# Attention heads in a one-core transformer step: transposing the probabilities of head i-1 ahead of the scores of head i

## The chip, the cores and the metric

The kernel runs on one core of a Trainium2 chip. The metric is the device time of one execution in microseconds. The engines are named as the profile names them: PE is TensorE's matrix multiplication (PEld its weight load), DVE is VectorE, ACT is ScalarE, POOL is GpSimd, and SP is SyncE, which here only issues transfers. A queue name such as ACTq is the engine's sequencer.

## What is computed

One step of a backbone with two layers, float32 throughout. It has 128 prompt tokens (block 0) and 512 sample tokens (blocks 1 to 4 of 128 each), and both groups go through both layers. A layer is a mixer, which holds two kinds of attention, and an expert stage:

```python
q_na, k_na, v_na, p, q_mla, ckv, krope = branch_inputs(h, lp)
o_na  = nat_latent_attn(q_na, k_na, v_na, kc_na, vc_na, rel_bias)   # sample: window + 128 cached keys
o_mla = dense_block_attn(q_mla, concat([k_lat, k_ctx]), concat([v_lat, v_ctx]), MLA_QK ** -0.5)
x = x + g1 * (concat([o_na, o_pool, o_mla]) @ w_out)
h2 = modulate(rms_norm(x, norm2), sh2, sc2)
x = x + g2 * peer(h2, peer_wq, peer_subkeys, peer_u, peer_v)
```

Each attention has six heads. `mla` (latent) attention lets each of the 512 sample tokens see all 512 sample keys and 128 cached ones, so 640. `na` (neighbourhood) attention lets a sample block see the neighbouring blocks of keys and the cached one: 384 keys for blocks 1 and 4, 512 for blocks 2 and 3, with a bias and a mask added. The prompt sees only its own 128 keys in both. Softmax is exact: a maximum over the row, an exponential with its sum, and a division at the end. In `peer`, eight heads choose 16 of 16384 experts for each token. For every block, head and choice one row of `peer_u` and one of `peer_v` (4 KB each, for each of 128 tokens) are gathered from memory. There are 1280 such steps, called rows below.

## The kernel before

**One order for all engines.** `whole_order` (from line 352) writes the whole work as one list of steps, `plan`. Each engine walks this list and does its own part of each step, with semaphores between the engines. What stands later in the list never overtakes what stands earlier on the same engine.

**The expert rows.** A step `("row", r)` makes POOL gather row r+4 of `peer_u` and row r-16 of `peer_v` (line 931), four buffers each. DVE multiplies a `u` row with the tokens and sums it (L1604), and does one part of a later unit's top-k search. ACT scales a 128x128 identity by the weights (L1192, 18 rows behind). PE multiplies this diagonal with the `v` row of 20 rows before and adds it up in `expert_sum` (L1933, four matmul records). Every 16 rows (a unit) ACT also computes a gelu (L1182), and PE a score product for a later unit (L1909).

**The weave.** `weave` (line 322) mixes the mixer's steps between the rows. It gives each step an estimated cost and spreads the sum of costs evenly over the rows. `s` and `pt` have the same cost (1.0), `pv` has 0.6. Rows 51 to 73 hold the sample's latent heads and the neighbourhood heads of block 1 in layer 0, rows 704 to 720 those of layer 1. Neighbourhood heads of blocks 2 to 4 stand in rows 84 to 116 and 728 to 759. The prompt's heads stand ahead of all rows in layer 0, blended with modulation products (L1661), and one step at a time between rows 432 and 497 in layer 1.

**A head of attention** is three steps.
- `s`: PE computes the scores (`scores`, L1820, two products for 640 keys). DVE adds bias and mask (L1415 and L1419, `na` of the sample only) and takes the maximum (L1424). ACT computes the exponential with its sum into `prob` in SBUF (L1137), which frees the scores' bank.
- `pt`: PE transposes the probabilities, one 128x128 transposition for each key block (`turn_probs`, recorded at the helper's L1635). They go in one part, or for 640 keys in part 0 (four blocks) and part 1 (the fifth). DVE copies part 0 of the sample's latent heads (L1436), ACT copies all other parts (L1149) to `prob_T`.
- `pv`: PE multiplies the transposed probabilities with the values (`head_values`, L1850). Behind a block's sixth head DVE divides by the sums (L1446, L1449).

`prob` and `prob_T` have two buffers each. `attention` (line 265) puts the heads' steps in order.

**The PSUM banks.** `work` has four banks. `Banks.place` (line 129) walks the plan and gives each result one bank, or the pair (0, 1) or (2, 3) for scores of 640 keys. Among the spots that are empty at that point of the plan it takes the one that has been empty longest. PE waits for the previous holder of the bank to be freed before it writes (`empty`). A bank counts as empty for the plan once the step that uses it has passed, though the engine may still be reading it. `pv` holds one bank for all six heads of a block.

Of the kernel before, what the change touches and what calls it, by code (L numbers as in the profile page):

```python
# [264 lines left out]
def attention(l, items):  # L265

    out = []
    for i in range(len(items) + 2):
        if i < len(items):
            out += [("s", l, *items[i])]  # L270
        if 1 <= i <= len(items):
            out += [("pt", l, *items[i - 1])]
        if i >= 2:
            out += [("pv", l, *items[i - 2])]
    return out
# [62 lines left out]
def prompt_mixer(l):  # L338
    att = attention(l, items_of("mla", GROUP[0]) + items_of("na", GROUP[0]))
    return heads_of_prompt(l), att  # L340


def sample_front(l):
    return (norm1(l, 1) + heads_of_sample(l) + attention(l, items_of("mla", GROUP[1]))
            + [("lX", l, b) for b in GROUP[1]] + attention(l, items_of("na", TAILS[1])) + tail(l, 1))
# [1683 lines left out]
```

## Time and profile before

| | |
|---|---|
| median of 3 runs | 4815.94 us (4813.23 to 4818.26) |
| profiled execution | 4793.14 us, span 4791.3 us |
| granted TensorE clock, mean | 0.949 of full speed |
| PE busy | 3804.4 us (79%) |
| DVE busy | 2559.7 us (53%) |
| ACT busy | 963.8 us (20%) |
| POOL busy | 2571.6 us (54%) |
| chain that ended last | PE 41%, POOL 19%, DMA 19%, issue 12%, DVE 4%, ACT 2% |

The span is the profiled execution from its first to its last instruction. Busy time is time in which an engine worked, so the rest of its span is waiting or issuing. The chain is followed back from the last instruction: at each step to what released it, or to the instruction before it on its engine. A share is thus the part of the span in which that engine was what all else waited for. Since the stages have different limits, the rows below are by stage. The times in them are microseconds from the start of the span.

### The profile page before, as it was taken

How to read it: one execution, taken by the hardware profiler on the slowest of the kernel's cores; microseconds unless marked ns; L12 is line 12 of the kernel's file. 1: busy time of each engine (PE TensorE's matmuls, PEld its weight loads, DVE VectorE, ACT ScalarE, POOL GpSimd, SP SyncE). 2: the span in 40 equal slices, each digit the busy share in tenths (PEclk: the TensorE clock that was granted, in tenths of full speed). 3: DMA queues.
4: the chain of work that ended last, by engine and by line, in shares of the span. 5: the costliest groups of instructions: out<-in, count | busy, mean ns of one | idle time of the engine just before them, and what ended most of it. 6: DMA issues, size and time to landing. Idle time of an engine off the chain costs nothing.

```text
span 4791.3 us, 37649 instructions
## 1 busy us (share of the span) xinstructions
PE 3804.4 (79%) x10586; PEld 1719.4 (36%) x10586; DVE 2559.7 (53%) x6434; ACT 963.8 (20%) x2482; POOL 2571.6 (54%) x2833
## 2 busy tenths in 40 slices
PE   7877789998888787778777958899977777777777
PEld 2344455443232233333223435554422222222222
DVE  1253456654555556655564334475565666666552
ACT  1122222221111112211121112231211121111111
POOL 0045324555666666666664441255566666666665
PEclk8988899999999999999999978899999999999999
DMA  5565658889999999999997534598999999999998
GB/s 197 209 217 172 194 177 329 319 312 370 382 392 385 382 393 365 369 366 374 378 371 275 184 129 155 188 347 311 330 370 370 365 373 367 371 370 367 367 368 303
DMA packets 464499, 1505.24 MB, mean 314 GB/s; under 512 B 59908, under 2 KB 78632, under 8 KB 463784
## 3 DMA queue, kind: packets, MB, share of 16 engines
q0 software_dynamic: 368640, 1342.34, 75.3%
q1 hardware_dynamic: 95656, 160.50, 9.6%
q8 instruction: 90, 1.47, 0.1%
q14 instruction: 113, 0.93, 0.1%
HBM read 1496.99 MB, written 5.67 MB: 314 GB/s over the span
## 4 chain that ended last, share of the span: by engine, by line
PE 41%; POOL 19%; DMA 19%; issue 12%; DVE 4%; ACT 2%; another core or an unknown queue 2%; SPq 1%; DVEq 0%; ACTq 0%; POOLq 0%
PE expert_sum L1933 20%; POOL expert_rows L931 17%; DMA expert_rows<-in_peer_v,experts 13%; DMA expert_rows<-in_peer_u,experts 5%; PE work L1687 4%; PE work L1661 3%; PE work L1884 3%; PE work L1899 3%; PE work L1820 2%; PE work L1635 2%; PE work L1850 2%; POOL stat_rstd L878 1%; DVE expert_rows L1604 1%; PE work L1872 1%
## 5 line engine op out<-in xcount | busy, mean ns | idle before, releaser
L1933 PE MATMUL expert_sum<-expert_rows,weight_diagonals 128*128 128x512 f32 x5120 | 2548.3, 628 | 676.4 <-DMA expert_rows<-in_peer_v,experts 501.5
L1604 DVE CUSTOM_DVE_ANT_0 expert_rows<-expert_rows,tokens 128x1024 f32<-128x1024 f32 x1280 | 1559.0, 1218 | 1098.8 <-DMA expert_rows<-in_peer_u,experts 971.4
L931 POOL DMA_INDIRECT expert_rows<-in_peer_v,experts x1280 | 1223.4, 956 | 1379.3 <-PE expert_sum L1933 970.4
L1933 PEld LDWEIGHTS expert_sum<-expert_rows,weight_diagonals 128*128 128x128 f32 x5120 | 928.1, 197 | 2073.9 <-issue 1911.9
L931 POOL DMA_INDIRECT expert_rows<-in_peer_u,experts x1280 | 1213.7, 948 | 476.3 <-issue 355.6
L1192 ACT ACTIVATE weight_diagonals<-ident,expert_weights 128x128 f32<-128x128 f32 x1280 | 437.2, 391 | 611.2 <-issue 260.0
L1635 PE MATMUL work<-ident,scratch 128*128 128x128 f32 (+1 forms) x814 | 156.8, 320 | 237.1 <-DVE scratch L1274 69.2
L1687 PE MATMUL work<-weight_ring,h_or_mixed 128*128 128x384 f32 (+2 forms) x800 | 260.6, 480 | 4.2 <-DMA weight_ring<-in_w_in 2.4
L1635 PEld LDWEIGHTS work<-ident,scratch 128*128 128x128 f32 (+1 forms) x814 | 112.4, 159 | 312.4 <-DVE scratch L1274 77.9
L1687 PEld LDWEIGHTS work<-weight_ring,h_or_mixed 128*128 128x128 f32 x800 | 147.8, 196 | 115.9 <-issue 61.9
L1182 ACT ACTIVATE gelu_dots<-dots 128x16 f32<-128x16 f32 x80 | 17.3, 216 | 847.6 <-issue 428.6
L1661 PE MATMUL work<-weight_ring,silu_cond 128*2 128x512 f32 x384 | 176.5, 615 | 13.2 <-DMA weight_ring<-in_w_mod 11.7
L875 POOL TENSOR_SCALAR stat_biased<-stat_sums 128x6 f32<-128x6 f32 (+1 forms) x82 | 16.9, 207 | 311.0 <-DVE stat_sums L1293 115.2
L1424 DVE TENSOR_REDUCE neg_max<-work 128x1 f32<-128x640 f32 (+3 forms) x120 | 76.3, 637 | 180.5 <-PE work L1820 168.9
L1899 PE MATMUL work<-h_or_mixed,weight_ring 128*128 128x128 f32 (+1 forms) x768 | 149.6, 354 | 3.7 <-ACT h_or_mixed L1010 3.7
L1137 ACT ACTIVATE scratch<-work,neg_max 128x640 f32<-128x640 f32 (+3 forms) x120 | 77.3, 644 | 353.3 <-DVE neg_max L1424 295.0
L1884 PE MATMUL work<-weight_ring,scratch 128*128 128x512 f32 x320 | 140.6, 592 | 0.0
L1899 PEld LDWEIGHTS work<-h_or_mixed,weight_ring 128*128 128x128 f32 x768 | 112.9, 200 | 49.0 <-issue 19.4
L1176 ACT ACTIVATE topk<-topk 128x16 f32<-128x16 f32 x80 | 24.5, 306 | 482.5 <-issue 254.4
L1604 DVE DVE_READ_ACCUMULATOR2_ANT dots<- 128x1 f32 x1280 | 105.5, 82 | 0.0
L1461 DVE COPY scratch<-work 128x512 f32<-128x512 f32 x20 | 13.8, 692 | 163.1 <-PE work L1884 163.1
L1182 ACT ACT_TABLE_LOAD x78 | 100.1, 1283 | 1.4
(164 smaller groups left out, 2591.1 us busy)
## 6 DMA issues: line engine op xcount, KB each, us to landing
weight_ring<-in_w_mod SPq DMA_DIRECT2D x24, 2048.0 KB
weight_ring<-in_w_out SPq DMA_DIRECT2D x12, 2048.0 KB
weight_ring<-in_peer_wq SPq DMA_DIRECT2D x12, 2048.0 KB
expert_rows<-in_peer_u,experts POOLq DMA_INDIRECT x1280
expert_rows<-in_peer_v,experts POOLq DMA_INDIRECT x1280
weight_ring<-in_w_in SPq DMA_DIRECT2D x12, 1536.0 KB
weight_ring<-in_w_in SPq DMA_DIRECT2D x4, 2048.0 KB
weight_ring<-in_t_pool SPq DMA_DIRECT2D x4, 2048.0 KB
```

The source lines that it names most:

```text
L931: g.indirect_dma_start(ring[row % n], None, table, bass.IndirectOffsetOnAxis(ap=idx_st[:, col:col + 1], axis=0),).then_inc(row_in[row % n] ...
L1182: a_.activation(gel[:, e * TOPK:(e + 1) * TOPK], dots[:, e * TOPK:(e + 1) * TOPK], ACT.Gelu_apprx_tanh).then_inc(gelu_ready, 1)
L1192: a_.activation(diags[:, at * P:(at + 1) * P], ident[:, :], ACT.Copy, scale=wgt[:, col:col + 1]).then_inc(diag_ready, 1)
L1604: v_.tensor_tensor_reduce(out=u_ring[r % U_RING], in0=u_ring[r % U_RING], in1=tokens[:, :], scale=1.0, scalar=0.0, op0=ALU.mult, op1=ALU.a ...
L1635: ins = t_.transpose(dst[0:n, j * P:(j + 1) * P], v, ident[:, :])
L1661: ins = t_.matmul(dst[0:2, :], sct[:, :].rearrange("p (c k) -> p k c", c=2)[:, kk, :], wt[:, kk, :], start=kk == 0, stop=kk == KC - 1)
L1687: ins = t_.matmul(dst[:, 0:n], hT(b, kk), wt[:, kk, 0:n], start=kk == 0, stop=kk == KC - 1)
L1820: ins = t_.matmul(dst[:, col:col + n], lhs, keys[:, key0:key0 + n], start=True, stop=True)
L1850: ins = t_.matmul(dst[:, h * DH:(h + 1) * DH], prob_T[item_no[item] % 2][:, k, :], val, start=k == 0, stop=k == len(blocks) - 1)
L1884: ins = t_.matmul(dst, o_T[:, kk, :], wt[:, kk, :], start=kk == 0, stop=kk == KC - 1)
L1899: ins = t_.matmul(dst[:, 0:len(blocks) * P], wt[:, kk, (h % 4) * P:(h % 4 + 1) * P], h_blocks[:, blocks[0]:blocks[-1] + 1, kk, :], start=k ...
L1933: ins = t_.matmul(acc[:, hf * 512:(hf + 1) * 512], diags[:, at * P:(at + 1) * P], v_ring[row % V_RING][:, hf * 512:(hf + 1) * 512], start= ...
```

## The change

In `attention`, the step `pt` of head i-1 is put ahead of the step `s` of head i. It stood behind it. `pv` of head i-2 stays last. All engines that take part in these steps (PE, DVE, ACT) walk the new order. The planner `Banks` and the weave run on the new list.

```diff
     for i in range(len(items) + 2):
+        if 1 <= i <= len(items):
+            out += [("pt", l, *items[i - 1])]
         if i < len(items):
             out += [("s", l, *items[i])]
-        if 1 <= i <= len(items):
-            out += [("pt", l, *items[i - 1])]
         if i >= 2:
             out += [("pv", l, *items[i - 2])]
```

## Rows read from the trace of the kernel before

**Rows 1.** Windows by stage; columns in the first line, PEclk is the clock.
```profile
core 0: us, PE busy (x) PEld busy (x) DVE busy (x) ACT busy (x) POOL busy (x), PEclk, DMA share, GB/s
550.00:682.00 132.00, 106.39 (x529) 70.48 (x528) 67.11 (x139) 36.94 (x96) 34.09 (x36) 0.96 0.53 177
682.00:705.00 23.00, 22.36 (x120) 15.22 (x119) 17.59 (x45) 8.15 (x25) 9.47 (x10) 1.00 0.83 296
1100.00:2550.00 1450.00, 1140.75 (x2707) 449.77 (x2707) 849.58 (x2203) 278.88 (x729) 921.38 (x975) 0.97 0.99 377
2895.00:3032.00 137.00, 111.24 (x526) 75.01 (x525) 58.52 (x118) 33.33 (x91) 26.25 (x28) 0.86 0.42 136
3117.00:3214.00 97.00, 97.00 (x400) 57.33 (x398) 82.02 (x195) 36.98 (x96) 58.50 (x62) 1.00 0.96 352
```
**Rows 2.** Chain of waits, a latent round: start, duration, engine, result and line.
```profile
2959.75 0.84 DVE neg_max L1424
...
2961.61 0.33 PE work L1635
2961.94 1.07 PE work L1850 x10
2963.01 1.15 PE work L1820 x4
...
2964.18 0.84 DVE neg_max L1424
```
**Rows 3.** The same view, latent rounds with an expert row in layer 0.
```profile
574.16 1.72 PE expert_sum L1933 x4
575.88 0.55 PE work L1635 x5
...
578.66 0.84 DVE neg_max L1424
...
584.83 0.83 DVE neg_max L1424
...
590.98 0.84 DVE neg_max L1424
```
**Rows 4.** The same view: a copy-out behind a turn, and scores started from idle.
```profile
565.48 0.34 PE work L1635
...
565.90 0.28 ACT scratch L1149
...
661.11 1.33 PE work L1820 x4
```
**Rows 5.** The same view, neighbourhood heads of block 1, both layers.
```profile
684.15 0.86 PE work L1820 x7
...
687.36 0.55 PE work L1635 x3
...
703.24 1.77 PE expert_sum L1933 x4
...
3033.28 0.86 PE work L1820 x7
...
3056.78 2.19 PE work L1850 x12
```
**Rows 6.** The same view, neighbourhood heads of blocks 2 to 4, both layers.
```profile
766.30 1.07 PE work L1820 x4
...
769.38 1.28 ACT L1137
...
771.51 0.66 PE work L1635 x4
...
3133.31 0.84 PE work L1850 x8
...
3135.21 1.91 PE expert_sum L1933 x4
3137.12 0.44 PE work L1635 x4
```
**Rows 7.** The same view, prompt heads of layer 0 beside a modulation product.
```profile
162.66 0.30 DVE neg_max L1424
...
163.55 7.04 PE work L1661 x16
```

## The prediction

> **What bounds the kernel now.** I read the windows by stage first [rows 1]. Most of the span (1100 to 2550 us, and again after 3380) is paced by the expert rows' transfers: DMA share 0.99 with TensorE at 79%. The change touches only stages where heads of attention are computed, and these differ. The neighbourhood heads of sample blocks 2 to 4 fill TensorE: 97.00 of 97 us in layer 1. Those of block 1 do so in layer 0 (22.36 of 23 us). The latent (mla) heads of the sample leave it 20% idle with DMA share only 0.42 to 0.53. The prompt's heads of layer 0 stand between modulation products of 7 us [rows 7]. Then I read the chain of waits inside each stage.
>
> In a latent head the chain is serial [rows 2]: the max starts 0.02 us after the scores end, the first transposition stands 1.86 us later (max, exponential), then one transposition 0.33, ten value matmuls 1.07, the next scores 1.15: a round of 4.43 us. Only one transposition stands in the chain, because head i-1's fifth key block is turned into a PSUM bank that scores(i) hold (the planner has four banks; the value sum keeps one for six heads, scores of 640 keys take a pair). So part 1 of turn i-1 waits for exponential i, although its data has long been there. The other four transpositions run under the max.
>
> In the neighbourhood heads scores fit one bank, two heads are in flight, and the chain is TensorE alone. Each head gives it scores 1.06, transpositions 0.44, values 0.84, and rows of 1.72 to 1.91 us between [rows 6].
>
> **The change, part by part.** No instruction, transfer or wait is added or removed. All engines walk the same plan, so DVE (max, copy-out of part 0), ScalarE (exponential, copy-out) and TensorE all get the new order; SP and POOL have no attention step, and rows, gathers and weight loads keep their order. What changes is which wait stands in TensorE's queue ahead of scores(i): the turn of head i-1, hence exponential i-1. Only one head is then in flight: exponential i-1, turn i-1, scores i, max i, exponential i. What can hide that latency is what stands between scores(i) and turn(i): values i-2 and whatever expert row the weave puts there.
>
> *Latent heads, round without a row.* By the planner's rule scores(i) now take the pair in which part 1 of turn i-1 lies, so they wait for its copy-out. The trace of before has the copy, not this wait: 0.28 us, starting 0.08 after the turn's end, and about 0.04 to the reader: 0.40 [rows 4]. Bounds are 0 (hidden behind a row) and 0.73, if the last transposition's 0.33 has to be paid once more on top. I take 0.40, the same kind of hand-over. Scores started from idle take 1.33 for 1.15 [rows 4]. New round: 1.88 window, 0.77 turn (0.33 plus four strides of 0.11), 0.40, 1.33 = 4.38, with the values inside the window. Against 4.43 that is nothing: 0.05 a head, 20 heads a layer, -1.0 us a layer.
>
> *Latent heads, rows.* Before, a row between scores and turn is free (round 4.50 from 574.16 to 578.66); one after the turn or after the values costs all of itself (6.17 and 6.15 for 4.43) [rows 3]. After, a row between turn and scores replaces the copy wait and the restart: 1.72 - 0.58 = 1.14. A row in the window makes 1.91 + 1.06 = 2.97 of TensorE work against 1.88; the turn then needs 0.55 for 0.77: +0.80 (it was free or 1.73). Walking the plan from head 3 of block 1: layer 0 had 9 full-price rows and the double row at 63 and 64 (with a score product, 2.2): 18.0 us. It now has 4 of 1.14, 9 of 0.80 and the double at 3.3: 15.1. Layer 1 had 7 full and 5 free: 12.4; now 5 and 7: 11.3. So -2.9 and -1.1. The end (values 3 now run in a window): -1.2 each. The start: before, three score products ran ahead; now heads 0 to 2 are serial, with no bank wait yet: 14.4 us to the scores of head 3 for 10.65, about +3.8 in each layer. Latent sum: -1.3 and +0.5, together -1 us (from -10 to +8: layer 1's stage was granted 0.86 and layer 0's 0.96 [rows 1], and it took as long with five rows fewer, some 8 us; when the lower of the two levels, 1.2 and 2.4 GHz, is granted I can't foresee).
>
> *Neighbourhood heads, block 1.* From scores' end (685.01) to the turn is 2.35 us [rows 5]. Layer 0, laid out by the plan: scores 0.86, turn 0.55, values 0.62 a head; windows of 2.35 for heads 0, 1, 3 and 4 hold at most 0.62; those of heads 2 and 5 hold a row and are covered; two rows stand after a turn (1.72 each). Scores and turns 8.2, four open windows 9.4, two covered ones 5.0, rows after a turn 3.4, the last values 1.3: 27.3 us against the 19.1 measured (684.15 to 703.24, where the next row begins): +8. Layer 1, in the same way with five open windows (one with a table load), one covered, and two rows and a score product after a turn: 29.2 at full clock, 25.7 measured (3033.28 to 3058.97) with parts at half clock: between +3.5 and +7, I take +6. Bounds from 0 (all hidden) to 17.
>
> *Neighbourhood heads, blocks 2 to 4.* Scores' end 767.37, turn 771.51, table load 1.29 of it: the window is 2.85 us for four key blocks [rows 6], and 2.35 for the three of block 4. The plan puts a row in every window. With values that is 2.6 to 2.75: 0.1 to 0.24 idle plus the turn's start from idle (0.66 for 0.44): 0.4 us for each of 7 heads in layer 0 and 9 in layer 1. Windows with two rows and those of block 4 cost nothing. The first two heads have no values to put in: 2.2 and 2.3. ScalarE reloads the exponential's table behind each gelu, twice a layer, 1.28 us; hidden now, since TensorE has other heads' work; then in the loop: +2.5 each. Sum: +7.5 and +8.4, together +16, with perhaps +2 where a row's heavier top-k step makes DVE late. The Trainium skill (ScalarE: Activation LUTs, What ACT_TABLE_LOAD costs) puts a table load at about 2.7 us; the trace has 1.28 [rows 6]. By the page's figure these four loads would cost 5.7 us more; the trace's duration is used.
>
> *Prompt heads.* Layer 0: the windows are 0.9 us (scores' end 162.63 to 163.55 [rows 7]), five are covered by modulation products of 7 us, and the chain already waits there now; +0.5 (0 to 4). Layer 1: one step between rows that the transfers pace; the row hides it: 0 (up to 12 x 0.9 = 11 without it).
>
> **Sum:** +0.5 prompt, -1 latent, +14 block 1, +16 blocks 2 to 4 = +30 us (rounded), all in stages that TensorE paces and ahead of transfer-paced ones that can't catch up with rings of four rows. On the profiled execution: 4791.3 span to 4821, and 1.8 us lie around it. That execution was 22.8 us under the median of the runs shown, so the forecast is 4815.94 + 30 = 4846 us.
>
> **The rivals.**
> *The clock falls (slower still).* The stages that are full now are granted full speed (1.00), those with 20% idle 0.86 and 0.96 [rows 1]. If the new idle brings the neighbourhood stages to 0.85, the TensorE work in them (97 and 22 us a layer, 238) grows by 0.17: 40 us, part of it in idle. About +30 on top: 4876. Against: in the largest stage 92% busy would remain (97 of 105). The Trainium skill (TensorE: Matmul & The Clock Gate, A second HAM failure mode: psum-queue depth-cycling) says that short idles between matmul groups while banks are cycled make the clock alternate; the trace agrees for the latent stages.
> *The transfers pace the neighbourhood stages (smaller loss).* DMA share is 0.96 there [rows 1]. At the 377 GB/s of the long stage a row (1.05 MB) takes 2.78 us, the 33 rows 92 of 97 us. If landings were what really paces, half the idle would be free: +14, 4830. Against: the chain shows no landing in that stretch.
> *Faster: the copy-out is covered.* Place: the latent heads. If turn part 1's copy is back before TensorE gets to the scores, and the turn starts without its idle start, the round is 4.38 - 0.40 - 0.18 - 0.22 = 3.6: 0.8 us off for about 42 heads, -35. With block 1's loss at its lower half (+7) and the clock of layer 1's latent stage back to full (-8) it ends at about -10: 4806. It decides from a round below 3.7 us. Against: the copy can't start before the turn ends, and the scores' pair includes its bank.
> *It doesn't do what it says:* banks are dealt out anew, so part 1 might wait for something else and the orders cancel: within 5 us of before.
>
> **How the numbers follow.** Main case 64%, 4846 (4827 to 4862). Clock 13%, 4876. Transfers 11%, 4830. Copy covered or cancelled 12%, 4800 to 4826. The range of 8 in 10 reaches into the clock's case and to the lower end of the main one: 4818 to 4880. Slower and faster count beyond 0.2% (9.6 us), about what a measurement of this kernel can tell from no change: slower 0.81, within 0.12 (3 from the main case, 4 from transfers, 5 from cancelling), faster 0.07.
>
> **What would show it.** Latent rounds without a row at 4.3 to 4.5 us, with all five transpositions, a copy of 0.28 and scores in the chain, values out of it. In blocks 2 to 4, max and exponential in a chain that is TensorE alone now, idle before the turn of 0.1 to 0.25, and more than 1.2 once behind each table load. Block 1 of layer 0 at 27 us for 19. Wrong if the latent stages are shorter than 115 us, or if blocks 2 to 4 stay at 100% TensorE.

## The result, and the profile after

The changed kernel takes 4864.88 us (median of 4 runs, 4856.44 to 4865.32) against 4814.58 us (4 runs, 4810.32 to 4818.26) for the kernel before on the same chip: a ratio of 1.0101, 95% interval 1.0083 to 1.0118, or 49 us more (40 to 57). The forecast was 30 us more, 4846 us. The profiled execution took 4864.57 us, with a span of 4862.8 us and a mean granted clock of 0.944. Each ratio below is to the kernel before, run beside the kernel named (4783.36 us for e1 to e4, 4791.90 for e5 to e7, 4783.21 for e10 and e11). One execution of e5 (10449.69 us) and one of the kernel before beside it (5481.69 us) ran at a granted clock of 0.38 and 0.68, and the ratios leave them out.

First the share of busy time, from the page of the kernel after:

```profile
PE 3840.1 (79%) x10586; PEld 1730.8 (36%) x10586; DVE 2560.8 (53%) x6434; ACT 970.2 (20%) x2482; POOL 2572.2 (53%) x2833
```

TensorE's busy time rose by 36 us, though no instruction was added. That already says that a part of the loss isn't waiting: some products took longer, because they ran at the lower clock or started from idle.

To compare stages, both traces were cut at the same work: the starts of VectorE's expert rows, counted from 0 to 1279, whose order the change doesn't touch. Rows 52 to 69 enclose the latent heads of the sample in layer 0, 69 to 74 block 1's neighbourhood heads, 84 to 117 those of blocks 2 to 4; in layer 1 these are 704 to 717, 717 to 728 and 728 to 760. Here are the windows of these six stages in the kernel after, in this order (columns in the first line):

```profile
core 0: us, PE busy (x) PEld busy (x) DVE busy (x) ACT busy (x) POOL busy (x), PEclk, DMA share, GB/s
558.90:691.20 132.30, 111.14 (x503) 72.12 (x502) 65.51 (x132) 37.35 (x96) 33.00 (x34) 0.90 0.51 172
691.20:734.10 42.90, 35.08 (x120) 21.68 (x119) 17.96 (x46) 8.78 (x26) 9.48 (x10) 0.68 0.48 156
777.60:912.20 134.60, 126.93 (x531) 76.36 (x531) 86.16 (x210) 43.60 (x110) 66.71 (x71) 0.94 0.85 301
2935.90:3073.10 137.20, 112.37 (x546) 73.68 (x545) 61.96 (x121) 36.31 (x93) 27.95 (x30) 0.94 0.46 151
3073.10:3149.30 76.20, 60.65 (x201) 35.60 (x200) 33.93 (x86) 15.94 (x38) 17.61 (x20) 0.82 0.55 194
3149.30:3272.20 122.90, 117.93 (x524) 71.35 (x523) 84.23 (x203) 41.94 (x107) 63.75 (x68) 1.00 0.90 318
```

The same six in the kernel before, cut at the same rows (the stretches of [rows 1] have other ends):

```profile
553.90:680.90 127.00, 101.39 (x503) 67.04 (x502) 64.06 (x133) 36.93 (x96) 32.20 (x34) 0.96 0.53 178
680.90:704.00 23.10, 22.46 (x120) 15.32 (x119) 17.68 (x46) 8.16 (x26) 9.47 (x10) 1.00 0.80 283
747.50:866.60 119.10, 117.92 (x527) 72.89 (x527) 85.98 (x210) 41.64 (x109) 66.30 (x71) 1.00 0.92 336
2886.60:3032.20 145.60, 119.84 (x546) 78.15 (x545) 60.17 (x121) 35.86 (x93) 27.64 (x29) 0.87 0.44 140
3032.20:3100.00 67.80, 57.31 (x202) 33.60 (x201) 33.73 (x85) 15.52 (x38) 17.50 (x20) 0.85 0.63 223
3100.00:3215.30 115.30, 115.30 (x525) 72.36 (x524) 84.36 (x203) 40.01 (x107) 63.23 (x68) 1.00 0.94 341
```

Read each pair of lines in two steps: the length less PE busy is what TensorE waits; PE busy is the same work in both, so where it grows, the clock fell (or a product started from idle). Block 1 of layer 0 waits 0.6 us before and 7.8 after, and its busy time goes from 22.5 to 35.1 at a granted clock of 0.68 for 1.00. Of the 20 us lost there, 7 are waiting and 13 are longer products. The turns started from idle before as well (0.55 for three key blocks in [rows 5]), so nearly all of the 13 are clock.

All stage lengths in one table (us, worked out from the starts of the rows; a kernel's name says what is in the new order):

| kernel | to row 0 | 52-69 | 69-74 | 84-117 | 432-500 | 704-717 | 717-728 | 728-760 |
|---|---|---|---|---|---|---|---|---|
| before | 241.3 | 127.0 | 23.1 | 119.1 | 194.8 | 145.7 | 67.8 | 115.3 |
| after | 244.7 | 132.3 | 42.8 | 134.6 | 197.3 | 137.2 | 76.2 | 123.0 |
| e1 latent | 237.4 | 129.0 | 23.1 | 119.8 | 194.7 | 141.1 | 66.2 | 115.1 |
| e2 neighbourhood | 238.4 | 127.0 | 41.2 | 132.1 | 194.8 | 146.4 | 77.2 | 122.9 |
| e3 block 1 | 240.5 | 127.0 | 41.3 | 120.2 | 193.8 | 146.3 | 77.2 | 115.3 |
| e4 blocks 2-4 | 241.1 | 127.0 | 23.1 | 127.1 | 193.8 | 138.7 | 67.9 | 122.9 |
| e5 block 1, filled | 237.9 | 127.0 | 34.9 | 121.3 | 193.9 | 146.3 | 70.1 | 113.8 |
| e10 block 1, filled x4 | 240.7 | 127.0 | 43.9 | 120.5 | 193.8 | 138.7 | 78.7 | 116.2 |
| e6 all, part 1 first | 244.4 | 117.3 | 40.8 | 129.6 | 194.6 | 132.7 | 77.2 | 122.9 |
| e7 latent, part 1 first | 241.0 | 117.3 | 23.0 | 121.7 | 194.7 | 132.8 | 67.5 | 114.7 |
| e11 old, part 1 first | 239.8 | 162.9 | 24.6 | 119.8 | 195.2 | 168.7 | 67.6 | 114.1 |

After minus before in these eight columns is +54 us. The rest of the two spans differs by another 18, nearly all of it (14.6) in the transfer-paced rows 760 to 1279, which took 1540.9 us in this execution and 1520 to 1528 in the profiles of before and of e1 to e11. Two of those, e6 and e8, have all heads in the new order and took 1524.3 and 1524.5. So that part belongs to the execution or its chip and not to the change, and the medians don't show it.

Column 704 to 717 holds a warning. It took 145.7 us before and 137.2 after, but e4 and e10, in which the latent heads keep the old order, took 138.7. The same instructions take 7 us more or less there from one profile to the next, with the clock. This line of e4 stands against 145.60 us at 0.87 before:

```profile
2898.30:3037.00 138.70, 111.80 (x547) 72.93 (x546) 60.19 (x122) 35.86 (x93) 27.64 (x30) 0.94 0.45 147
```

Next the chain of waits after (start, duration, engine, result, line), in a latent round of layer 1 without a row, the counterpart of [rows 2]:

```profile
2979.06 0.79 DVE neg_max L1424
...
2979.93 0.89 ACT scratch L1137 x2
...
2980.87 0.78 PE work L1635 x5
...
2981.73 0.29 ACT scratch L1149
...
2982.06 1.36 PE work L1820 x4
...
2983.45 0.83 DVE neg_max L1424
...
2985.32 0.76 PE work L1635 x5
```

From turn to turn 4.45 us (2980.87 to 2985.32). The first max row is cut short: it shows 0.79 us, because the chain enters this max only where VectorE's piece before it ends, so the 4.39 from max to max is a little low. By the starts of the instructions themselves, six rounds of this kind in layer 1 take 4.43 to 4.46 us from max to max. The prediction had 4.38, and before it was 4.43. Window 1.90 (1.88 forecast), turn 0.78 (0.77), copy-out with both hand-overs 0.41 from 2981.65 to 2982.06 (0.40), scores 1.36 (1.33). The values have left the chain, and one serial round has replaced another of the same length.

Block 1 of layer 0, the counterpart of [rows 5]:

```profile
694.51 0.86 PE work L1820 x4
...
697.73 0.90 PE work L1635 x3
698.63 3.41 PE expert_sum L1933 x4
702.05 1.59 PE work L1820 x4
...
705.97 0.90 PE work L1635 x3
```

The scores end at 695.37 and the turn starts at 697.73: the window is 2.36 us, as forecast (2.35). But the turn then takes 0.90 for 0.55, the row 3.41 for 1.72 and the scores 1.59 for 0.86: these instructions ran at 1.2 GHz, the lower level. Blocks 2 to 4 of layer 0, the counterpart of [rows 6]:

```profile
797.46 1.07 PE work L1820 x4
...
800.54 1.28 ACT L1137
...
802.67 1.12 PE work L1635 x4
...
811.72 1.07 PE work L1820 x4
...
815.63 0.66 PE work L1635 x4
...
892.77 3.69 another core or an unknown queue
```

Between scores and turn stand 2.84 us (812.79 to 815.63), with a table load 4.14 (798.53 to 802.67). The turn behind this load is at half clock again. The last line is a wait of VectorE whose releaser the profile doesn't name. It isn't the change's: the same wait stands in the last nine rows of this stage in e5 (3.82 us), e7 (3.76) and e11 (3.07), where these heads keep the old order, and not in the profiles of before, e2, e4 and e6.

### The profile page after: what moved, and what is told of

It is laid out like the page before. It is cut to its first block, busy times and chain, and to the rows that moved or that the text cites. A ratio compares the mean times of both kernels' runs of the same rounds, so it can differ in the third digit from the quotient of the medians.

```text
span 4862.8 us, 37647 instructions
## 1 busy us (share of the span) xinstructions
PE 3840.1 (79%) x10586; PEld 1730.8 (36%) x10586; DVE 2560.8 (53%) x6434; ACT 970.2 (20%) x2482; POOL 2572.2 (53%) x2833
## 4 chain that ended last, share of the span: by engine, by line
PE 39%; POOL 21%; DMA 16%; issue 13%; DVE 5%; ACT 3%; another core or an unknown queue 3%; SPq 1%; ACTq 0%; DVEq 0%; POOLq 0%
POOL expert_rows L931 19%; PE expert_sum L1933 18%; DMA expert_rows<-in_peer_v,experts 11%; DMA expert_rows<-in_peer_u,experts 5%; PE work L1687 4%; PE work L1661 3%; PE work L1884 3%; PE work L1899 2%; PE work L1635 2%; PE work L1820 2%; ACT scratch L1137 1%; POOL stat_rstd L878 1%; PE work L1850 1%; DVE expert_rows L1604 1%
## 5 line engine op out<-in xcount | busy, mean ns | idle before, releaser
L1137 ACT ACTIVATE scratch<-work,neg_max 128x640 f32<-128x640 f32 (+3 forms) x120 | 77.3, 644 | 300.7 <-DVE neg_max L1424 244.6
L1424 DVE TENSOR_REDUCE neg_max<-work 128x1 f32<-128x640 f32 (+3 forms) x120 | 76.4, 637 | 114.7 <-PE work L1820 107.8
```

The lines of the kernel that those rows point to most:

```text
L1137: a_.activation(prob[i % 2][:, 0:n], src[:, 0:n], ACT.Exp, bias=nmax[:, i % 2:i % 2 + 1], accum_out=rsum[:, at:at + 1]).then_inc(banks.fre ...
```

## The experiments

Each kernel selects in which group of heads the new order holds: `attention` gets a third argument, and the callers pass True where the text says so.

```
-def attention(l, items):
+def attention(l, items, turn_first=False):
...
+        if turn_first and 1 <= i <= len(items):
+            out += [("pt", l, *items[i - 1])]
         if i < len(items):
             out += [("s", l, *items[i])]
-        if 1 <= i <= len(items):
+        if not turn_first and 1 <= i <= len(items):
             out += [("pt", l, *items[i - 1])]
```

**One group at a time.** The first four ran together, beside the kernel before at 4783.36 us.

e1: latent heads of the sample, `attention(l, items_of("mla", GROUP[1]), True)`.

> Only the sample's latent heads (blocks 1 to 4, both layers) take the new order; the neighbourhood heads and the prompt keep the old one. My theory (a round without a row is 4.38 us for 4.43, the start of a stage loses 3.8, rows and the end give it back): the same as before, -8 to +8 us. The rival, that the copy-out is covered and a round falls below 3.7 us: -25 to -35 us. The rival that the loss of the whole change lies here (the score product waits for a bank): +30 to +50 us.

Measured: ratio 0.9999 (0.9985 to 1.0014), no change. The latent heads neither pay nor gain.

e2: the neighbourhood heads of the sample, `items_of("na", TAILS[1])` and `items_of("na", TAILS[2])`.

> Only the sample's neighbourhood heads (blocks 1 to 4, both layers) take the new order. If the loss comes from one head in flight in stages that TensorE filled, nearly all of it is here: +42 to +52 us. If the change's cost lay in the latent heads, or in what the prompt's part moves behind it: +5 to +15 us.

Measured: 1.0110 (1.0079 to 1.0141), 53 us more (the medians alone: 49), as much as the whole change. The loss is in the neighbourhood heads.

e3: block 1 of them alone, `items_of("na", TAILS[1])`.

> Only the neighbourhood heads of block 1 take the new order (6 heads a layer). By the sum in the prediction, without any change of the clock: +14 us. If the clock falls in the stage, as the trace of the changed kernel shows it (the stage from row 69 to row 74 of layer 0 is 19.7 us longer, layer 1's 8.2): +24 to +30 us.

Measured: 1.0057 (1.0039 to 1.0075), 27 us more; 18.2 in rows 69 to 74 and 9.4 in 717 to 728. Twelve of the 120 heads make half of the 53 us. The window of rows 69 to 74:

```profile
681.70:723.00 41.30, 33.48 (x119) 20.59 (x118) 17.93 (x46) 8.78 (x26) 9.46 (x10) 0.75 0.50 166
```

Waiting is 7.8 us for 0.6 before, and busy time 33.5 for 22.5 at a clock of 0.75: the same two parts as in the kernel after.

e4: blocks 2 to 4 alone, `items_of("na", TAILS[2])`.

> Only the neighbourhood heads of blocks 2 to 4 take the new order (18 heads a layer). By the prediction's sum: +16 to +18 us. If late expert rows on VectorE ahead of the heads' maxima add to it, as 23 us between rows 84 and 117 and between 728 and 760 of the changed kernel's trace suggest: +20 to +26 us. If the transfers paced these stages all the same: 0 to +8 us.

Measured: 1.0026 (1.0009 to 1.0043), 12 us more (the medians alone: 16). By stage 8.0 and 7.6, which is the forecast's 7.5 and 8.4. The 16 to 18 us expected lie within the interval (4 to 21 us) and agree with the stages' 15.6. The interval alone doesn't exclude the transfer rival's 0 to 8; the stages do.

**Is it the clock?** e5 is e3 with one product more ahead of each of block 1's turns, put in the window in which TensorE has nothing to do:

```
                 item = (l, kind, b, h)
+                if kind == "na" and b == 1:
+                    dst = empty(("pt", *item, 0))
+                    for _ in range(1):
+                        t_.matmul(dst[:, :], ident[:, :], mpp[:, :], start=True, stop=True)
                 pe.wait_ge(*banks.freed(("s", *item)))
```

> New order in block 1's neighbourhood heads alone, as in the run that cost 27 us (12 heads), and ahead of each of these heads' turns TensorE makes one product of 512 columns more (identity times the mask, into the bank that the turn then overwrites), about 0.25 us at full clock and 0.45 at half: 12 x 0.25 = 3 us of added work, placed in the window in which TensorE has nothing to do. Theory (the open windows lower the granted clock, and that is what the first block's stage lost beyond the 8 us of the plan): with part of each window filled the stage of layer 0 is granted a higher clock and takes less than the 38 us of the unfilled run (from 28 to 35), although it holds more work. Rival 1 (the stage is long by waits alone, the clock only goes with it): the product lies in idle time and changes nothing, 37 to 39 us. Rival 2 (TensorE's own time is what counts): each product delays the turn, 40 to 43 us.

Measured: 1.0036 (1.0022 to 1.0049), 17 us more than before. Window of rows 69 to 74, and the chain in it; L1822, L1637 and L1939 are the scores, turns and rows, L1830 the added product:

```profile
677.00:711.90 34.90, 31.02 (x131) 18.36 (x130) 17.88 (x46) 8.74 (x26) 9.47 (x10) 0.95 0.59 200
```
```profile
680.28 0.86 PE work L1822 x4
...
683.49 0.55 PE work L1637 x3
684.04 1.72 PE expert_sum L1939 x4
685.76 0.86 PE work L1822 x4
...
708.39 0.91 PE work L1830 x2
...
711.16 0.91 PE expert_sum L1939 x2
```

The window is still 2.35 (681.14 to 683.49), but turn, row and scores are back at 0.55, 1.72 and 0.86. The stage is 6.4 us shorter than e3's (41.3, where the expectation had 38), and layer 1's 7.1, although each holds six products more. An added product costs 0.91 us (two records in the trace, x2), not the 0.25 that was expected, so this is all the clearer. The rival by which the clock only goes with the waits is out: more work in the same waits made the stage shorter. From the first scores (680.28) to the row behind (711.16) are 30.9 us; two products lie outside open windows and are paid (0.91 above and one of 1.12), which leaves 28.9, where the forecast for a full clock was 27.3.

e10: four such products (`range(4)`).

> As the filled run of block 1's heads, with four products of 512 columns ahead of each of the twelve turns for one (4 x about 0.22 = 0.9 us of work in a window of 2.35 that holds 0.62 of values and nothing else). With one product the stage from row 69 to row 74 of layer 0 was granted 0.95 and took 34.9 us, with none 0.75 and 41.3, before the change 1.00 and 23.1. Theory (only the clock is at stake, the windows stay waits): the clock goes to 0.97 to 1.00, the added products lie in the wait, and the stage takes 32 to 35 us, by which the waits alone are worth 9 to 12 us. Rival (added work is paid): 5 heads x 3 x 0.22 = 3.3 us more than with one product, 38 us or longer.

Measured: 1.0082 (1.0053 to 1.0111). Window of the same rows, then the group of the added products (busy, mean ns of one, idle before):

```profile
680.20:724.20 44.00, 43.98 (x168) 24.95 (x167) 17.96 (x46) 8.81 (x26) 9.50 (x10) 1.00 0.50 168
```
```profile
L1830 PE MATMUL work<-prompt_pooling,ident 128*128 128x512 f32 x48 | 22.0, 600 | 0.0
```

Against the expectation, because that rested on 0.22 us a product: 22.0 us for 24 of them is 0.92 each, 3.7 in a window of 2.35. TensorE is full and granted 1.00, and what is left of its busy time, 43.98 - 22.0 = 22.0, is the 22.5 us of work that the kernel before has there. So it shows that the work didn't grow in the new order, and that the 11 us by which e3's busy time (33.48) lies above it come with the open windows, as lower clock in the main. It doesn't show what the waits alone cost; for that e5 is the nearest.

**The copy-out in the latent rounds.** e6: the kernel after, with part 1 of each turn first:

```
-                for part, (lo, hi) in enumerate(turn_parts(kind, b)):
+                for part, (lo, hi) in reversed(list(enumerate(turn_parts(kind, b)))):
                     transposes(("pt", *item, part),
...
-            return ("pt", *item, len(turn_parts(*item[1:3])) - 1)
+            return ("pt", *item, 0)
```

> The changed kernel, but in every turn of head i part 1 (the fifth key block of a latent head, whose bank the scores' pair needs) is transposed first and the four of part 0 after it, so that the copy-out of part 1 runs under the other four transpositions (4 x 0.11 us) and the scores of the next head don't wait for it. Heads of the neighbourhood have one part and don't change. Theory (the copy-out of 0.40 us and the restart from idle of 0.18 stand in each latent round): a round without a row falls by 0.4 to 0.6 us, 40 heads of which about half have no row in the way: 15 to 25 us less than the changed kernel, that is about +20 to +35 us against before. Rival (something else is late by as much: the copy of part 0, or the max): within 8 us of the changed kernel, +42 to +57 against before.

Measured: 1.0051 (1.0034 to 1.0067), 24 us more than before for the change's 49. The chain of a round:

```profile
2950.09 0.73 DVE neg_max L1424
...
2950.90 0.89 ACT scratch L1137 x2
...
2951.93 0.74 PE work L1635 x5
2952.67 1.35 PE work L1820 x4
...
2954.05 0.84 DVE neg_max L1424
...
2956.01 0.74 PE work L1635 x5
```

The copy is gone from the chain, and scores follow the turn without a gap: 4.08 us from turn to turn (2951.93 to 2956.01) for 4.45, 0.37 less. The copy's 0.41 has gone, and the turn starts 0.1 us later behind the exponential. Both latent stages shorten, by 15.0 and 4.5 us. Not all of that is the copy. The window of rows 52 to 69:

```profile
557.00:674.30 117.30, 101.12 (x503) 67.16 (x502) 65.48 (x133) 37.43 (x96) 33.11 (x34) 0.97 0.57 192
```

Waiting fell from 21.2 to 16.2 us, and busy time from 111.1 to 101.1 at a clock of 0.97 for 0.90: 5 us of the 15 are waits and 10 are clock. So the total fell within the expected 15 to 25 us, but the expectation had no clock in it.

e7: the same edit, with the new order in the latent heads of the sample alone.

> New order in the latent heads of the sample alone (that cost nothing by itself), with part 1 of each turn transposed ahead of part 0 for every head; prompt and neighbourhood heads keep the old order. Theory (the copy-out stands in the chain): the new order's latent round loses 0.4 to 0.6 us of 4.4 and the kernel is 15 to 25 us faster than before, less if transfers pace the stage. Rival (round is set by max, exponential and scores, with a copy that was hidden anyway): within 5 us of before. A third possibility: in the old order the prompt's heads are now slower or faster by their bank order, at most 4 us by the row that starts behind them.

Measured: 0.9945 (0.9929 to 0.9961), 26 us faster than before: the version that beats both kernels. The latent stages took 117.30 and 132.70 us:

```profile
553.60:670.90 117.30, 101.18 (x503) 67.21 (x502) 65.47 (x132) 37.43 (x96) 33.12 (x34) 0.97 0.58 192
2872.60:3005.30 132.70, 112.57 (x546) 74.41 (x545) 61.93 (x121) 36.30 (x93) 28.06 (x29) 0.92 0.48 156
```

The whole gained a little more than the 15 to 25 us expected. In layer 0 the busy time is that of before (101.2 and 101.4), and the 10 us come out of waiting alone. In layer 1 waiting fell by 5.6 us; the other 7 us that this stage is shorter than before are no more than it varies by itself.

e11: part 1 first in the old order, nothing else.

> The kernel before in its own order of heads, with part 1 of each turn transposed ahead of part 0, and nothing else. It tells whether the 26 us that the new order in the latent heads gained with part 1 first come from the part's place alone. Theory (they need both: in the old order part 1 waits for the exponential of the next head, since that head's scores hold its bank, and part 0's four transpositions, which ran under the max, now stand behind that wait): four strides of 0.11 us more in each round, 0.44 us, for the 20 heads a layer without a row behind the scores some 10 to 18 us slower than before. Rival (part 1 first gives the gain by itself): 10 to 26 us faster than before.

Measured: 1.0122 (1.0094 to 1.0150), 58 us slower. So the gain needs both edits. The sign is as expected, the size is not, and the window of rows 52 to 69 and two rows of the chain say why:

```profile
551.90:714.80 162.90, 129.68 (x503) 86.05 (x502) 65.33 (x133) 36.95 (x96) 32.20 (x34) 0.78 0.41 139
```
```profile
563.54 1.30 PE work L1635 x5
564.84 2.03 PE work L1850 x10
```

Waiting grew from 25.6 to 33.2 us, by 7.6 (in layer 1 from 25.8 to 33.3, by 7.5): together 15, within the 10 to 18 expected. Busy time grew by 28.3 at a clock of 0.78; ten value products take 2.03 for 1.07. The turn of all five blocks stands behind the exponential, as expected, and the clock put about three times the waiting on top.

**The table load.** e8 and e9 leave gelu out of the kernels after and before (the hidden values are copied), so that the exponential's table stays loaded:

```
-ACT.Gelu_apprx_tanh
+ACT.Copy
```

> The changed kernel with gelu's function left out (the expert rows' hidden values are copied), so that ScalarE needn't load the exponential's table again behind each gelu. To be held against the same edit of the kernel before, stage by stage. Theory (each reload of 1.28 us in a neighbourhood window is paid in full in the new order and was hidden in the old): the stretch of blocks 2 to 4 (rows 84 to 117 and 728 to 760), which the change lengthened by 8.0 and 7.5 us where only these heads were in the new order, is lengthened by 5 to 6 us in each layer, 2 x 1.28 less. Rival (TensorE has other work during the reload): lengthened by 7.5 to 8 as with gelu.

> The kernel before with gelu's function left out in the same way, as the base for the changed kernel without it. In the neighbourhood stages, where TensorE is busy without a gap, the reload of the table is hidden: rows 84 to 117 take 119.1 us and rows 728 to 760 115.3 as in the kernel before, within 1 us.

Measured, one profile each, rows 84 to 117 and 728 to 760, e9 and then e8:

```profile
748.40:866.40 118.00, 118.00 (x529) 73.05 (x528) 86.09 (x210) 35.12 (x104) 66.26 (x71) 1.00 0.93 340
3090.20:3204.20 114.00, 114.00 (x513) 71.08 (x513) 84.30 (x203) 34.65 (x102) 62.78 (x67) 1.00 0.93 342
```
```profile
765.30:889.10 123.80, 121.34 (x531) 73.81 (x531) 86.09 (x210) 37.25 (x105) 66.88 (x71) 1.00 0.90 324
3113.80:3234.00 120.20, 117.62 (x521) 71.03 (x520) 84.22 (x203) 36.58 (x102) 63.86 (x68) 1.00 0.91 325
```

Without the loads the change costs 5.8 and 6.2 us there, with them (e4) 8.0 and 7.6: 2.2 and 1.4 us for 2.5 each. Fair agreement, no more: e8 has all heads in the new order and e4 only these, and single profiles differ by about 1 us here. e9's own stages are 1.1 and 1.3 us shorter than those of before, slightly more than the 1 us expected, so a little of the load may have been paid in the old order too. Layer 0's stage, 134.6 us in the kernel after, is granted 1.00 in e8 and 0.94 there.

**The prompt's heads.** e12: `attention(l, items_of("mla", GROUP[0]) + items_of("na", GROUP[0]), True)` alone. This one ran on a chip on which the kernel before takes 4607.73 us, since the transfer-paced stages are shorter there (rows 760 to 1279 take 1415 us in e12, for 1520 to 1541 in all the others).

> New order in the prompt's heads alone (the twelve heads of block 0, in both layers). To be read by stage: in the ten kernels whose prompt heads keep the old order VectorE's first expert row starts 237.4 to 241.3 us after the span's start, in the three that have all heads in the new order at 244.3 to 244.7; rows 432 to 500, which hold the prompt's heads of layer 1, take 193.8 to 195.2 us in the former and 197.3, 196.8 and 194.6 in the latter. Theory (the prompt's heads pay for the new order in layer 0): first row at 243.5 to 245, rows 432 to 500 within 193.8 to 197.3, all later stages as before, the whole within 6 us of before plus what one execution differs from another. Rival (the prediction's 0.5 us, the rest is how executions differ): first row at 241.8 or earlier.

Measured: 4603.63 us, a single run, 4.1 us less than the single run of the kernel before; single runs of the kernel before on one chip differ by up to 25 us (4772.50 to 4797.04), so the whole decides nothing. Row 0 starts at 244.6 us, where the kernels with the old order in these heads have 237.4 to 241.3, 239.9 in the mean: about 4.6 us are paid in layer 0, at least 3.3. The stages between rows 52 and 117 are as before (127.0, 23.1, 119.1). Rows 432 to 500 took 176.3 us and can't be compared across chips.

## Why the prediction was right, and where it was short

The direction, the place and most of the waits were right; what it left too small is the clock. 4864.88 us lies just above the main case's own bounds (4827 to 4862). It is inside the whole range because that reached up into the clock's case.

- **Latent round, 4.38 us.** It came out at 4.43 to 4.46, each term within 0.03 us; the 0.05 a head that it was to gain didn't come. A round with a row between turn and scores was to be 4.38 + 1.14 = 5.52 us, and the trace after has 5.46 (max at 612.74 and at 618.20). That the scores wait for part 1's copy is shown by e6, where the copy leaves the chain.
- **Latent sum, -1 (from -10 to +8).** e1 measures 0 for both layers. Of single stages: -1.3 was forecast for layer 0, and it was +2.0 in e1 and +5.3 in the kernel after, with 4.5 us less waiting in both (25.6 before, 21.1 and 21.2 after) and 6.5 and 9.8 more busy time, at a clock of 0.92 and 0.90 for 0.96. Layer 1's -8.5 can't be put down to the change: e4 and e10 have 138.7 without it. So the sum of -1 agrees with e1 partly by luck: the stage of layer 0 lost where it was to gain, through a clock that the sum didn't have, and layer 1's varies by more than what was forecast.
- **Block 1, +8 and +6.** This term was mis-sized: +19.7 and +8.4 (in e3 +18.2 and +9.4). Its own sum has a small slip (six scores and six turns are 8.5 us, not 8.2), which changes nothing. The open windows are there, 2.35 us each, and the waiting in layer 0 grew by 7.2 us, as forecast. What the step lacked was that 12.6 us of busy time would follow. The text put this on a rival that it gave 13% and priced for the neighbourhood stages as a whole (0.85 everywhere, 30 us). In fact it split: 0.68 in block 1 of layer 0, 0.94 and 1.00 in the large stages. The argument against it, that the largest stage would still be 92% busy, was true of that stage, where a row fills nearly every window, and said nothing of the small one with its open windows. e5 shows that the clock is a cost of its own: with a product of 0.91 us in each window 6.4 us come back.
- **Blocks 2 to 4, +7.5 and +8.4.** Alone +8.0 and +7.6: right, with window 2.84 for 2.85 and table load 1.28 in the chain, where e8 and e9 make it worth 2.2 and 1.4 us a layer (2.5). The load takes 1.28 us in the trace after too. The Trainium skill (ScalarE: Activation LUTs, What ACT_TABLE_LOAD costs) makes its 2.7 us out of about 1.28 for the load itself and 1.38 for a drain, so the prediction held the page's total against the trace's load. The load agrees with the page. The drain isn't seen: a window with a load is 4.14 us for 2.84, 1.30 more, and the measurement decides. In the kernel after layer 0 has +15.5. Of the 7.5 us that are not in e4, 2.7 are in its first eight rows (49.4 us at 0.92; e4 46.7 at 0.96), as in e2 and e6, where block 1 is in the new order too, and 4.8 in the last nine (31.4 us at 0.89; e4 26.6 at 1.00), with the wait of 3.69 us that isn't the change's. Why the clock is low in the first part there isn't settled. Block 1's stage in the new order lies ahead of it in all three kernels, but in e8 too, where these eight rows took 46.0 us at 0.99 without table loads.
- **Prompt, +0.5 (0 to 4).** It was +3.4 in layer 0 (1.4 of it waiting, 2.0 busy time), and e12 shows about 4.6, at least 3.3: this term was too small, at the upper end of its bounds or just beyond. Which windows are paid stays open. Layer 1: +2.5 in the kernel after, -0.2 in e6.
- **What the rivals came to.** The clock came true in part, as said. Transfers don't pace these stages. The covered copy, the faster rival, was to decide at a round below 3.7 us; the kernel after has 4.45. With e6's edit the copy is covered and the round is 4.08: 0.37 off for the 0.40 priced, but the turn (0.74 for 0.55) and the scores (1.35 for 1.15) keep the starts from idle that this rival took off as well. It didn't happen in the change itself, and took an edit of its own. Its price was also added up wrongly: -1, -35, -8, +7, +16 and +0.5 make about -20 us (4795), not the -10 (4806) that the prediction wrote, and its range of 4800 to 4826 didn't hold that.

The forecast's sum with block 1 and the prompt as measured is -1 + 28 + 16 + 3.5 = 46.5 us, for the 49 of the medians. That it comes so close is in part luck: it leaves out the 7.5 us more in blocks 2 to 4 of layer 0 and what the latent stages did, and the eight columns of the profiles add up to 54.

On the page of the Trainium skill that the prediction named for this (TensorE: Matmul & The Clock Gate, A second HAM failure mode: psum-queue depth-cycling): the rule that short idles between groups of matmuls make the clock alternate agrees with block 1's stage after and with e5, where filling a part of each idle brought the grant from 0.75 to 0.95. The page's case is another kernel, in bf16.

## What to carry to other kernels

Where a reorder opens waits of 2 us on TensorE in a stage that was full, price the stage twice: the waits, and then its own products at the lower clock; here the second was the larger (12.6 against 7.2 us) in the stage whose windows stood open, while the stages in which a row filled nearly every window kept 0.99 and 1.00 when they alone had the new order. A serial chain is not mended by changing which head comes first if the same bank still has to be copied out; look for the part whose result is needed first and issue that one first (0.37 us a round in e6), and use the order only for the heads that lack the banks to have two in flight (e7, 26 us faster than before). In the old order the same part first cost 58 us (e11). Compare stages at the same piece of work, and look at several profiles of one code before a difference of some us in a stage is put down to the change.

## What was not expected of the hardware

- In one and the same stage the granted clock followed no simple share of busy time: the latent stage of layer 0 was granted 0.96 with TensorE 80% busy (101.39 of 127.00 us) before, and 0.78 with 80% (129.68 of 162.90) in e11. The turns stand differently in the idle (behind the exponential in e11, mostly under the max before); whether that decides was not tested.
- Added work made a stage shorter: six products of 0.91 us each, 41.3 us before them and 34.9 with them.
- Unchanged code took 145.7 us at 0.87 or 138.7 at 0.94 in rows 704 to 717 of layer 1, in profiles of kernels that differ elsewhere.
- A product of 128x128 by 128x512 in float32 takes 0.91 us at full clock (two records, x2; 24 of them 22.0 us at a grant of 1.00 in e10), nearly four times the estimate on which two expectations rested.
